# A depthwise convolution of 31 taps moved wholly to the matrix engine, and its layer norm moved among the products of the memory projection

## What is computed

```
proj = h @ w_in                                  # h: rms-normed x, 256 x 1024
a    = proj[..., :768] + b_glu[:768]
gate = proj[..., 768:1536] + b_glu[768:]
q_mem = proj[..., 1536:]                          # 256 columns, 4 heads of 64
u = a * sigmoid(gate)
c[t, n] = sum over tap of u_pad[t + tap, n] * dw_w[tap, n]   + dw_b[n]     # 31 taps, 768 channels
c = silu(layer_norm(c, ln_g, ln_b))
m = memory_attention(q_mem, memq_g, mem_k, mem_v)            # mem_k, mem_v = rms_norm(mem) @ w_mem_kv
out = concatenate([c, m]) @ w_out
```

## Time and profile before

| | us |
|---|---|
| median of 3 runs | 2216.43 (2215.78 to 2218.17) |
| the profiled execution | 2214.42 |
| its span, first to last instruction | 2212.6 |
| PE busy | 2172.8 (98%) |
| DVE busy | 1719.5 (78%) |
| ACT busy | 1410.7 (64%) |
| POOL busy | 114.9 (5%) |

### The profile page before, as it was taken

One profiled execution on the slowest core, in us unless ns is written; L12 is line 12 of the kernel. 1 busy time (PEld: TensorE's weight loads), 2 busy tenths in 40 slices (PEclk: granted clock), 3 DMA queues, 4 the chain that ended last, 5 costly groups with the idle time before them and its releaser, 6 DMA issues.

```text
span 2212.6 us, 35919 instructions
## 1 busy us (share of the span) xinstructions
PE 2172.8 (98%) x11570; PEld 1843.4 (83%) x11570; DVE 1719.5 (78%) x2261; ACT 1410.7 (64%) x1884; POOL 114.9 (5%) x150
## 2 busy tenths in 40 slices
PE   8999999999999999999999999999999999999998
PEld 7889987778888888888888888787789888778987
DVE  7956657699999999999999999866576556657654
ACT  4264446578787888878787878745645444564543
POOL 8000004120000000000000000000010000001000
PEclk9999999999999999999999999999999999999999
DMA  5235554279999999999999999944445555444554
GB/s 215 96 115 191 180 190 163 77 267 367 349 368 377 358 356 353 381 355 351 356 372 365 368 358 354 344 169 146 140 167 189 191 190 185 148 140 169 179 199 143
DMA packets 151054, 551.99 MB, mean 249 GB/s; under 512 B 16736, under 2 KB 16864, under 8 KB 150752
## 3 DMA queue, kind: packets, MB, share of 16 engines
q1 hardware_dynamic: 150448, 548.77, 68.6%
q10 hardware_dynamic: 432, 1.02, 0.1%
HBM read 548.67 MB, written 1.05 MB: 248 GB/s over the span
## 4 chain that ended last, share of the span: by engine, by line
PE 87%; issue 7%; DVE 4%; ACT 1%; DMA 1%; POOL 0%; DVEq 0%; SPq 0%; ACTq 0%; POOLq 0%
PE L L2159 58%; PE L L2212 9%; PE L L2744 6%; PE L L2834 3%; PE TB L2227 2%; PE L L2176 2%; DVE cacc L1518 1%; PE SC L2415 1%; DVE wlo L1238 1%; PE TB L2317 1%; PE SC L2298 1%; PE L L2357 1%; PE SC L2626 1%; PE SC L2634 1%; PE L L2465 1%
## 5 line engine op out<-in xcount | busy, mean ns | idle before, releaser
L1238 DVE TENSOR_TENSOR wlo<-deep,whi 128x1024 fp32r<-128x1024 f32 x682 | 809.8, 1223 | 43.6 <-ACT whi L696 12.9
L696 ACT ACTIVATE whi<-deep 128x1024 fp32r<-128x1024 f32 x682 | 712.8, 1060 | 133.0 <-PE L L2159 130.7
L1238 DVE TENSOR_TENSOR wlo<-raw,whi 128x1024 fp32r<-128x1024 f32 x353 | 427.7, 1226 | 247.2 <-ACT whi L696 242.5
L696 ACT ACTIVATE whi<-raw 128x1024 fp32r<-128x1024 f32 x353 | 367.9, 1058 | 315.0 <-PE L L2159 154.8
L2159 PE MATMUL L<-whi,xhi 128*128 128x512 f32 (+1 forms) x1136 | 447.7, 394 | 2.8 <-DVE wlo L1238 2.4
L2159 PE MATMUL L<-whi,xlo 128*128 128x512 f32 (+1 forms) x1136 | 441.9, 389 | 0.0
L2159 PE MATMUL L<-wlo,xhi 128*128 128x512 f32 (+1 forms) x1136 | 441.5, 389 | 0.0
L2159 PEld LDWEIGHTS L<-whi,xhi 128*128 128x128 f32 x1136 | 213.6, 188 | 48.8 <-DVE wlo L1238 6.2
L2159 PEld LDWEIGHTS L<-whi,xlo 128*128 128x128 f32 x1136 | 213.7, 188 | 45.1
L2159 PEld LDWEIGHTS L<-wlo,xhi 128*128 128x128 f32 x1136 | 213.9, 188 | 42.1
L2159 PE MATMUL L<-whi,mhi 128*128 128x512 f32 x448 | 175.3, 391 | 0.0
(11 more groups left out here) (384 smaller groups left out, 3406.0 us busy)
## 6 DMA issues: line engine op xcount, KB each, us to landing
deep<-wm SPq DMA_DIRECT2D x679, 512.0 KB, 5.5
raw<-wm SPq DMA_DIRECT2D x245, 512.0 KB, 3.4
raw<-w SPq DMA_DIRECT2D x112, 512.0 KB, 4.3
mbuf<-mem SPq DMA_DIRECT2D x2, 1024.0 KB, 8.5
const<-const SPq DMA_DIRECT2D x1, 1312.0 KB, 7.7
out<-hn SPq DMA_DIRECT2D x2, 512.0 KB, 2.6
h<-x ACTq DMA_DIRECT2D x1, 512.0 KB, 4.8
h<-x SPq DMA_DIRECT2D x1, 512.0 KB, 4.6
```

Of the source, the lines that this page charges most:

```text
L696: act(hi, slots[:, slot, :], ACT.Copy).then_inc(w.s.hi, 1)
L1238: v.tensor_tensor(lo, slots[:, slot, :], hi.bitcast(F32), ALU.subtract).then_inc(w.s.lo, 1)
```

## The change

The convolution leaves DVE altogether. Channels are regrouped: a tile of 128 channels is four quarters `g` of 32. For each pair `c` an array `shifted[c]` is filled by DMA: its partitions `j*32 .. j*32+31` hold the 32 channels of quarter `g`, shifted by `j` columns (`j` = 0 to 3), so that a product over 128 partitions sums four taps of 32 channels. The weights `wst` are 128 x 32: four diagonal blocks of 32 x 32, one for each of four taps. Eight steps `m` make 32 taps (the last has weight 0). Each product's result goes to the 32 partitions of its quarter. That is 64 products for a pair (2 tiles x 8 steps x 4 quarters), where PE had 26 and DVE 36 instructions.

The copies are 48 DMAs of 32 partitions x 2 x 284 values (73 KB each), 16 for each pair, all issued on ACT's queue (`shifts`). The weights `wst` are made by POOL in three instructions over 2048 columns each. DVE only adds the bias on the way out (`convolved`). The layer norm's steps on PE are put ahead of panels 15, 16 and 17, the first panels of the output projection follow the projection of the memory, the scores come behind them, and the four filling products go.

The core of the diff (declarations of semaphores, the same regrouping of the weight table on the host and two memsets are left out):

```diff
-TAPS_PE = 13
-TAPS_V = TAPS - TAPS_PE
+QT, QC = 4, 32
+STEPS = 8
+SPAN = S + QT * (STEPS - 1)
...
-        diag = [sb(f"diag{k}", [P, TAPS_PE, P], F32, at) for k, at in enumerate(
-            (region + 45056, region + 52224, region + 1024, region + 11264, region + 33536, smx_at))]
+        shifted = [sb(f"shifted{c}", [P, QT, 2, SPAN], F32, at) for c, at in enumerate(
+            (region + 1024, region + 11264, region + 33536))]
+        wst = [sb(f"wst{c}", [P, 2, STEPS, QT, QC], F32, at) for c, at in enumerate(
+            (region + 45056, region + 53248, smx_at))]
+        spare = sb("spare", [P, D], F32, smx_at + 8192)
+        same = sb("same", [P, QC], F32)
...
-            def diagonals(c):
-                for i in range(TAPS_PE):
-                    for k in (2 * c, 2 * c + 1):
-                        ins = e.tensor_scalar(diag[k][:, i, :], ident, sp("dww", k * TAPS + TAPS_V + i, 1), 1.0, ALU.mult, ALU.mult)
-                ins.then_inc(s_diag, 1)
+            def tap_tiles(c):
+                e.tensor_tensor(wst[c][:, :, :, :, :].rearrange("p f m g n -> p (f m g) n"),
+                                sp("dww", 2 * c * STEPS * QT, 2 * STEPS * QT).unsqueeze(2).to_broadcast([P, 2 * STEPS * QT, QC]),
+                                same[:, :].unsqueeze(1).to_broadcast([P, 2 * STEPS * QT, QC]), ALU.mult).then_inc(s_wst, 1)
             row(w)
-            e.wait_ge(s_in[0], 16)
-            e.wait_ge(s_in[1], 16)
+            e.wait_ge(s_same, 1)
             for c in range(3):
-                diagonals(c)
+                tap_tiles(c)
             row(w)
             heads(w, 4)
+            power(s_ln, 1, stat[:, 8:8 + T], T, s_lnp)
             heads(w, 4, 48)
-            power(s_ln, 1, stat[:, 8:8 + T], T, s_lnp)
...
+            def shifts(c):
+                e.wait_ge(s_ev, c + 1)
+                for j in range(QT):
+                    for g in range(QT):
+                        e.dma_start(shifted[c][j * QC:(j + 1) * QC, g, :, :],
+                                    u[g * QC:(g + 1) * QC, 2 * c:2 * c + 2, j:j + SPAN]).then_inc(s_shift[c], 16)
...
+            chunk(w, 4, last)
+            sigmoids(0)
+            chunk(w, 4, last)
+            shifts(0)
+            sigmoids(1)
+            e.wait_ge(s_in[3], 16)
+            for t in range(T):
+                i = act((mkv[:, :, :].rearrange("p t n -> p (t n)"), spare[:, :])[t], mbuf[:, t, :], ACT.Square,
+                        accum_out=norm_cols(w)[:, t:t + 1])
+            i.then_inc(w.s.nss, 1)
+            w.n["n"] += 1
+            chunk(w, 4, last)
+            shifts(1)
+            sigmoids(2)
+            w.n["p"] += 2
+            w.n["g"] += 1
+            shifts(2)
+            head_squares(w, ((s_ev, 4), [(z[:, :, 0:256], PT[:, 0, 0, :].rearrange("p (t n) -> p t n", t=T))]))
+            e.wait_ge(w.s.used, w.at("p", SLOTS))
+            split_to(w, w.n["p"] + 2)
+            for q in range(4):
+                turned_group(w, q, lambda k: sp("mem_g", k, 1))
+                if q == 1:
+                    split_to(w, w.n["p"] + 4)
+            turned_heads(w, [(qkT[:, 0:2, :], 2, sp("cvq"))])
+            w.n["p"] += 4
+            w.n["g"] += 1
+            for c in range(3):
+                e.wait_ge(s_cen, c + 1)
+                act(u[:, 2 * c:2 * c + 2, 0:S], cacc[:, 2 * c:2 * c + 2, :], ACT.Square).then_inc(s_lsq, 1)
+            split_to(w, w.n["p"] + 2)
+            silus(0)
+            silus(1)
+            head_squares(w, ((s_ev, 5), [(mkv[:, :, 0:256], PT[:, 0, 1, :].rearrange("p (t n) -> p t n", t=T))]))
+            silus(2)
+            split_to(w, w.n["p"] + 3)
+            turned_heads(w, [(mkT, 2, sp("memk"))])
+            split_to(w, w.n["p"] + 4)
             def between(s):
-                if s < 0:
-                    silus(0)
-                elif s == 0:
-                    silus(1)
-                    silus(2)
-                else:
-                    split_to(w, w.n["p"] + min(2 * s + 2, 8))
+                if s >= 0:
+                    split_to(w, w.n["p"] + min(2 * s + 5, 8))
...
-            glu(0, tapped_chunk(0))
-            glu(1, tapped_chunk(4))
-            taps(2 * TAPS_V - 16)
...
+            def convolved(c):
+                e.wait_ge(s_tap, QT * (c + 1))
+                for f in range(2):
+                    k = 2 * c + f
+                    i = v.tensor_scalar(cacc[:, k, :], SC[c % 2][:, f * S:(f + 1) * S], sp("dwb", k, 1), None, ALU.add)
+                i.then_inc(s_conv, 1)
...
+            for c in range(3):
+                glu(c, chunk(w, 4, last))
             mean_square(w)
...
+            split_to(w, w.n["p"] + 2)
+            head_sums(w, PT[:, 0, 0, :].rearrange("p (t n) -> p t n", t=T), 32, 4)
+            convolved(0)
+            head_scale(w, z[:, :, 0:256], 32, 4, 0)
...
+                if q == 1:
+                    split_to(w, w.n["p"] + 4)
+                    convolved(1)
+            convolved(2)
+            turned_heads(w, [(qkT[:, 0:2, :], 2, sp("cvq"))])
...
-            def taps(c, begin, end):
-                e.wait_ge(s_ev, c + 1)
-                e.wait_ge(s_diag, c + 1)
+            def convolution(c):
+                e.wait_ge(s_shift[c], 16 * QT * QT)
+                e.wait_ge(s_wst, c + 1)
                 if c >= 2:
                     e.wait_ge(s_conv, c - 1)
-                for n in range(begin, end):
-                    f, i = n // TAPS_PE, n % TAPS_PE
-                    tap = TAPS_V + i
-                    ins = mm(SC[c % 2][:, f * S:(f + 1) * S], diag[2 * c + f][:, i, :], u[:, 2 * c + f, tap:tap + S],
-                             start=(i == 0), stop=(i == TAPS_PE - 1))
-                if end == 2 * TAPS_PE:
-                    ins.then_inc(s_tap, 1)
+                for f in range(2):
+                    for m in range(STEPS):
+                        for g in range(QT):
+                            ins = mm(SC[c % 2][g * QC:(g + 1) * QC, f * S:(f + 1) * S], wst[c][:, f, m, g, :],
+                                     shifted[c][:, g, f, QT * m:QT * m + S], start=(m == 0), stop=(m == STEPS - 1),
+                                     skip_group_check=True)
+                            if f == 1 and m == STEPS - 1:
+                                ins.then_inc(s_tap, 1)
             chunk_features(w, before=turn_rows(w, hn, (s_xr, 2)))
             chunk_features(w)
-            taps(0, 0, 2 * TAPS_PE)
             chunk_features(w)
             chunk_tokens(w, xhi, xlo, [4, 4], width=256, pitch=256)
-            chunk_tokens(w, xhi, xlo, FULL, before=turn_rows(w, mbuf, (s_in[3], 16)))
-            taps(1, 0, 2 * TAPS_PE)
+            convolution(0)
+            e.wait_ge(s_in[3], 16)
+            turn_group(w, mbuf, 0)
+            turn_group(w, mbuf, 1)
+            convolution(1)
+            turn_group(w, mbuf, 2)
+            turn_group(w, mbuf, 3)
+            convolution(2)
             e.wait_ge(A.zrdy, 1)
             turn(w, [(c * S + t * P, z[:, t, c * P:(c + 1) * P]) for c in range(2) for t in range(T)])
-            taps(2, 0, TAPS_PE)
-            e.wait_ge(A.zrdy, 2)
-            turn(w, [(c * S + t * P, mkv[:, t, c * P:(c + 1) * P]) for c in range(2) for t in range(T)])
-            taps(2, TAPS_PE, 2 * TAPS_PE)
-            e.wait_ge(w.s.tfree, w.at("t", 2))
             ones = co("ones")
             memory = mem_pairs(0)
-            e.wait_ge(s_conv, 2)
-            for k in range(FC):
-                if k == 4:
+            def layer_norm(panel):
+                if panel == 1:
                     e.wait_ge(s_conv, 3)
-                ins = mm(TB[0][:, 0:S], ones, cacc[:, k, :], start=(k == 0), stop=(k == FC - 1))
-            ins.then_inc(s_mean, 1)
-            attention(w, memory, SLOTS_MEM, scored=0)
-            for c in range(3):
-                e.wait_ge(s_lsq, c + 1)
-                for k in (2 * c, 2 * c + 1):
+                    for k in range(FC):
+                        ins = mm(SC[1][:, 0:S], ones, cacc[:, k, :], start=(k == 0), stop=(k == FC - 1))
+                    ins.then_inc(s_mean, 1)
+                elif panel == 2:
+                    for c in range(3):
+                        e.wait_ge(s_lsq, c + 1)
+                        for k in (2 * c, 2 * c + 1):
+                            for t in range(T):
+                                ins = mm(SC[0][:, S + t:S + t + 1], u[:, k, t * P:(t + 1) * P], ones[:, 0:1],
+                                         start=(k == 0 and t == 0), stop=(k == FC - 1 and t == T - 1), skip_group_check=True)
+                    ins.then_inc(s_lvar, 1)
+                elif panel == 3:
+                    e.wait_ge(w.s.tfree, w.at("t", 1))
+                    e.wait_ge(s_dg, 1)
                     for t in range(T):
-                        ins = mm(TB[1][:, S + t:S + t + 1], u[:, k, t * P:(t + 1) * P], ones[:, 0:1],
-                                 start=(k == 0 and t == 0), stop=(k == FC - 1 and t == T - 1), skip_group_check=True)
```

(73 more changed lines are left out.)

101 lines of the change are left out of this document (30 added, 71 removed).

## The result

The changed kernel takes 2224.6 us in the median of six runs (2221.8 to 2225.2), the kernel before 2216.75 in six runs beside it (2213.5 to 2218.4): a ratio of 1.0035, 95% interval 1.0025 to 1.0045. It is slower by 7.9 us, where 8 us less was forecast. The profiled execution has a span of 2222.9 us, 10.3 longer than that of before.

The account below looks back on a forecast made before the run. PE, 98% busy, was taken as the bound: only its path in the first 150 us counts. Last output panel 150.0 to 138.5, 11.5 less; 3.4 back for clock falls: -8.1, 2206.3 profiled, plus 2.0: 2208 us. Range 2202 to 2228.

Parts of the forecast that it names:

- The convolution, 33.7 out, 3 x 7.1 in: Convolution on PE: 156 tap rows of 33.7 us replaced by three pairs of 7.1 us, a gain of 12.4 us.
- Rivals 1 (9 to 11): Convolution on PE: quarters overlap only partly, 9 to 11 us a pair, total 2216; chance 0.13.
- 2 (13.8): Rival 2, convolution on PE: strict program order, only two rows together, 13.8 us a pair, total 2226; chance 0.15.
- The argument from the halved products: A later layer's 8 halved-product rows took 1.02 us, so halves run together; quarters were taken to do so four at a time.
- Three POOL products of 2048 columns: 0: Making the weights on POOL: 6 to 9 us each, at most 28, covered by chunks 1 and 2; 0 us added.
- I take 0.45: Copy issues on ACT: 0.45 us each, 7.2 us for sixteen; ends 5.3 and 8.6, from 0.33 and 0.54 an issue.
- rival 3: Copy issues on ACT back up at 0.7 to 1.0 us each: 12 us in all, 2220, or 2234; chance 0.10.
- The walk behind it: Step-by-step timing from panel 10's split to the last output panel: its end at 138.5 instead of 150.0 without clock falls.
- The holes of 2.8, 1.5 and 1.8: Attention: PE idle 2.8 us for panel splits behind transposes' copies; 1.5 and 1.8 at its end, DVE splitting among divisions.
- Two falls of the clock: PE, first 150 us: two falls to half clock as before, 1.7 us each, 3.4 us given back.
- DVE's taps go: 0: Convolution on DVE: 108 instructions of about 0.45 us leave, but they ran beside PE, so 0 us gained.
- the copies' landing 0: The shifted copies: 4.7 us a pair at 246 GB/s, landing before PE wants them, 0 us added.

Follow-up runs that it names:

- e6_order: e3_both with the convolution's two inner loops exchanged, all eight products of one quarter before the next: 2250.93 us, ratio 1.0156.
- e1_pieces: The changed kernel with each of POOL's three 2048-column products cut into eight pieces of 256: 2216.84 us, ratio 1.000 to the kernel before.
- e4_pool: The kernel before plus three unread POOL products of 128 x 2048 ahead of its diagonals: 2226.26 us, ratio 1.0045.
- e3_both: The changed kernel with POOL's products in eight pieces each and the copies' issues on SP: 2204.05 us, ratio 0.9948 to the kernel before.
- e9_pool: e3_both with later panels' splits moved forward and all 48 copy issues on POOL's queue behind its pieces: 2201.28 us, ratio 0.9923.
- e10_share: e3_both with later panels' splits moved forward, twelve issues of each set on SP and four on ACT: 2197.87 us, ratio 0.9918.

## Why the prediction was wrong

- **The convolution, 33.7 out, 3 x 7.1 in: right.** 7.11 us a pair at full clock in every kernel that goes round the quarters. Rivals 1 (9 to 11) and 2 (13.8) fall. The argument from the halved products held for quarters. The Trainium skill's figure in "TensorE: Matmul & The Clock Gate", Part 3, 2.38 times for three column tiles, would have made it 8.7 by the forecast's estimate; here four tiles gave 27.6/7.1 = 3.9 times. The "strict FIFO" of the same part of the Trainium skill is not what `e6_order` shows, where a row starts at 59.252 us ahead of three that stand before it, nor are free queues for each quarter.
- **"Three POOL products of 2048 columns: 0": wrong, the step that failed first.** They took 3.6 us each, less than the 6 to 9 reckoned, and ended at 21.7 us, well before 40. I asked only when PE wants their result, not what they share with DVE while they run. Their price is 7.8 us (`e1_pieces`), or 9.5 on the kernel before (`e4_pool`): some 5.8 us of start, and 2.2 for chunk 0 at half clock behind it. The 78 diagonals that they replaced were short pieces, 0.37 us alone. The 578 ns that the forecast read as POOL's price had POOL's waits for DVE in them: the effect lay in the trace that it was worked out from.
- **"I take 0.45" for an issue: wrong in size.** It was 0.66 to 0.74 by sets, above both my ends for this term, and what rival 3 had: 0.7 costs 12. Moving them to SP was worth 13.1 alone and 12.8 beside the pieces. The mechanism was as walked: waits at panel 11 and at the transposes. But they were 5.2 and 3.3 us instead of 2.2 and 1.2, and each was followed by a fall of the clock beyond the two counted. The 0.45 came from one issue with nothing ahead of it. Each DMA has its price whatever it moves.
- **The walk behind it: right, once these two are taken out.** It gave 142 for the last output panel with two falls, 3.4 us of it (2.2 and 1.2) for the issues. `e3_both` has neither loss and ends at 138.8, with two falls. The holes of 2.8, 1.5 and 1.8 in the attention and at its end were measured as 2.51, 1.39 and 1.11. The first output panel waited 0.9 instead of 0.6. Against before, `e3_both` gained 12.7, where 8.1 + 3.4 = 11.5 were reckoned.
- **Two falls of the clock: wrong, six.** Three (14.9, 59.3, 90.0) stand behind holes that the two losses made, two (137.8, 148.1) behind holes that I had named, one (110.5) behind the squares' one-column products. `e3_both` kept two, 3.4 and 6.8 us long, and had none behind the same squares.
- **"DVE's taps go: 0", "the copies' landing 0": right.** PE never waited on `shifted` in the changed kernel.
- The sum: -8.1 + 7.8 for the port + 12.8 - 3.4 for the issues is +9.1; +7.9 was measured. 2224.6 lay in the range, on the side of rival 3, whose chance of 0.10 was too small for a rate read from one lone issue, and the other half of the loss was in no rival.

## What to carry to other kernels

An instruction of POOL is not free because its result is wanted late: look at what DVE does meanwhile, and cut it into pieces as short as DVE's own, even if POOL then needs twice as long. Count DMAs, not bytes, on the queue that issues them: sixteen in a row held what stood behind them for some 11 us, so put them where nothing urgent stands behind, or share them out. When products on different columns are to run together, write them in turns, one of each.

## What the runs showed of the hardware that I had not expected

- POOL's products exclude DVE's cast, its `tensor_scalar` of 12 columns and its instructions with two inputs in SBUF, and those with two inputs exclude POOL's. One product of 2048 columns holds a DVE instruction of 12 columns for 3.61 us, and a piece of 256 columns takes POOL 1.6 us beside a `wlo` instead of 0.61.
- In rows of sixteen or more, an issue of a copy between partitions costs 0.64 to 0.74 us on average on SP and ACT, at 71 KB (the 73 of above, in units of 1024 bytes) and on SP at 35.5 KB alike, and 0.53 on POOL, where landing takes 7.5 us instead of 2.5.
- Rows of the convolution start ahead of up to three waiting ones (`e6_order`).
- Two kernels whose PE groups start alike from 94 to 118.4 us differ in the clock granted behind them, for over 13 us (`e9_pool`, `e10_share`). It need not be the kernel at all. The four executions of `e9_pool` took 2197.7, 2199.7, 2202.9 and 2203.5 us at a mean granted clock of 0.998, 0.998, 0.996 and 0.995: the same program runs longer at half clock in some executions than in others, and the profiled one was the slowest. What decides it stays open, and so the 3.4 us between the two are not put down to the queues.
